# Order of the first transfers, of VectorE's evacuations and of a few steps between experts in a two-layer hybrid trunk

## The reference, cut to what matters

```python
for l in range(DEPTH):                                   # DEPTH = 2
    h = rmsnorm(x, norm_mix[l])
    qa, ka, va, qb, kb, vb, qi, ki, wi, qc, kc, vc, g = split(h @ w_in[l])
    o_a, o_b, o_c = stick_breaking(...), indexed_top_k(...), sliding_window(...)
    gates = sigmoid(g + b_gate[l])
    merged = gates[0] * (o_a @ w_pa[l]) + gates[1] * (o_b @ w_pb[l]) + gates[2] * (o_c @ w_pc[l])
    x = x + merged @ w_out[l]
    x = x + cross_attention(rmsnorm(x, norm_x[l]), rmsnorm(mem, norm_mem[l]), ...)
    hf = rmsnorm(x, norm_ffn[l])
    x = x + (swiglu(hf, w_gu_dense, w_down_dense) if l % 2 == 0 else
             moe_swiglu(hf, w_router, w_gu_moe, w_down_moe))   # sum over 8 experts, top 2 per token
```

## Time and profile before

| | |
|---|---|
| median of 3 runs | 1813.37 us (1812.16 to 1819.61) |
| the profiled execution | 1814.6 us, of which the profile's span is 1813.0 us |
| PE busy | 1717.1 us, 95% of the span, mean granted clock 0.984 |
| DVE busy | 1405.6 us, 78% |
| ACT busy | 1112.3 us, 61% |
| POOL busy | 93.7 us, 5% |
| DMA | 498 MB, 275 GB/s over the span |
| experts (about 800 us to the end) | 56% of the span |

### The profile page before, as it was taken

One profiled execution on the slowest core, in us unless ns is written; L12 is line 12 of the kernel. 1 busy time (PEld: TensorE's weight loads), 2 busy tenths in 40 slices (PEclk: granted clock), 3 DMA queues, 4 the chain that ended last, 5 costly groups with the idle time before them and its releaser, 6 DMA issues.

```text
span 1813.0 us, 22257 instructions
## 1 busy us (share of the span) xinstructions
PE 1717.1 (95%) x7776; PEld 1373.4 (76%) x7776; DVE 1405.6 (78%) x1258; ACT 1112.3 (61%) x1006; POOL 93.7 (5%) x68
## 2 busy tenths in 40 slices
PE   6999887999989998879999989999999999999999
PEld 5877666788768676667888878888788888788776
DVE  5798675554477967748888878888888888888897
ACT  4646354444345453537777777777777777877765
POOL 1200000000003000010000000000000000000440
PEclk9999998999999999979999999999999999999999
DMA  8533592555445325409999989999999999999985
GB/s 288 206 107 135 189 349 93 186 184 185 162 140 204 134 104 186 186 22 397 365 361 380 366 314 387 364 380 368 346 390 362 369 387 366 367 362 366 402 328 203
DMA packets 73791, 498.13 MB, mean 275 GB/s; under 512 B 8192, under 2 KB 8960, under 8 KB 17552
## 3 DMA queue, kind: packets, MB, share of 16 engines
q1 hardware_dynamic: 66000, 466.55, 67.9%
q0 software_dynamic: 7328, 29.87, 4.6%
q10 hardware_dynamic: 416, 1.08, 0.2%
HBM read 481.73 MB, written 15.73 MB: 274 GB/s over the span
## 4 chain that ended last, share of the span: by engine, by line
PE 77%; DVE 11%; ACT 4%; issue 3%; DVEq 3%; DMA 2%; ACTq 0%; SPq 0%; POOLq 0%
PE ps L516 24%; PE ps L520 24%; PE ps L512 24%; DVE w_lo L397 3%; DVE w_lo L901 1%; ACT w_hi L392 1%; PE ps L701 1%; DMA raw<-in_layer_tiles 1%; PE ps L1201 1%; DVE hT_lo L505 1%; DVE st L1447 1%; ACT w_hi L831 1%; DVEq L1450 1%; ACT scratch L1366 0%; DMA z<-rows_of_experts 0%
## 5 line engine op out<-in xcount | busy, mean ns | idle before, releaser
L512 PE MATMUL ps<-w_hi,hT_hi 128*128 128x512 f32 (+1 forms) x1552 | 436.5, 404 | 33.6 <-ACT hT_hi L500 10.6
L901 DVE TENSOR_TENSOR w_lo<-raw,w_hi 128x2048 fp32r<-128x2048 f32 x168 | 391.3, 2331 | 64.2 <-ACT w_hi L831 64.2
L901 DVE TENSOR_TENSOR w_lo<-z,w_hi 128x2048 fp32r<-128x2048 f32 x168 | 386.6, 2305 | 57.1 <-ACT w_hi L831 56.1
L516 PE MATMUL ps<-w_hi,hT_lo 128*128 128x512 f32 (+1 forms) x1552 | 424.3, 396 | 0.8 <-DVE hT_lo L505 0.4
L520 PE MATMUL ps<-w_lo,hT_hi 128*128 128x512 f32 (+1 forms) x1552 | 422.2, 394 | 0.7 <-DVE w_lo L397 0.7
L512 PEld LDWEIGHTS ps<-w_hi,hT_hi 128*128 128x128 f32 x1552 | 278.8, 190 | 96.7 <-ACT hT_hi L500 12.5
L516 PEld LDWEIGHTS ps<-w_hi,hT_lo 128*128 128x128 f32 x1552 | 290.9, 189 | 73.0 <-DVE hT_lo L505 4.1
L831 ACT ACTIVATE w_hi<-z 128x2048 fp32r<-128x2048 f32 x168 | 321.3, 1915 | 39.9 <-PE ps L520 36.2
L520 PEld LDWEIGHTS ps<-w_lo,hT_hi 128*128 128x128 f32 x1552 | 291.0, 189 | 71.2 <-DVE w_lo L397 1.6
L831 ACT ACTIVATE w_hi<-raw 128x2048 fp32r<-128x2048 f32 x168 | 321.1, 1912 | 25.5 <-PE ps L520 25.5
L397 DVE TENSOR_TENSOR w_lo<-raw,w_hi 128x2048 fp32r<-128x2048 f32 (+2 forms) x111 | 243.5, 2203 | 105.0 <-ACT w_hi L392 104.5
(11 more groups left out here) (260 smaller groups left out, 977.5 us busy)
## 6 DMA issues: line engine op xcount, KB each, us to landing
z<-in_moe_tiles SPq DMA_DIRECT2D x168, 1024.0 KB, 6.5
raw<-in_moe_tiles SPq DMA_DIRECT2D x168, 1024.0 KB, 6.5
raw<-in_layer_tiles SPq DMA_DIRECT2D x68, 1024.0 KB, 4.9
raw<-in_dense_tiles SPq DMA_DIRECT2D x33, 1024.0 KB, 4.8
rows_of_experts<-z POOLq DMA_DIRECT2D x1, 8704.0 KB, 37.8
raw<-in_layer_tiles SPq DMA_DIRECT2D x8, 512.0 KB, 3.6
z<-rows_of_experts POOLq DMA_DIRECT2D x8, 512.0 KB, 10.2
rows_of_experts<-z POOLq DMA_DIRECT2D x7, 512.0 KB, 8.1
```

Source lines behind the costliest of these rows:

```text
L512: pe.matmul(acc, hi[:, k, cols], wh, start=start and j == 0, stop=False)
L516: pe.matmul(acc, lo[:, k, cols], wh, start=False, stop=False)
L901: v.tensor_tensor(w_lo[:, ring, :], moe_raw(p), w_hi[:, ring, :].bitcast(F32), ALU.subtract) \
```

## The change

- The identity goes first on SP's queue, then the left half of x's columns, slot 0, the right half, slots 1 and 2, the other five constants, the memory. ACT issues the gains alone. PE waits for the identity, then for each half of x ahead of its transposes, and for the other constants ahead of the fifth slot of `in`.
- In `dve_linear` and `dve_merge` the low halves go up to one slot less before tile 0's evacuation, and the last one stands between the evacuations of tile 0 and of tile 1.
- `dve_merge` signals the left half of the merged rows by its own semaphore; PE turns it without waiting for the right half.
- ACT's Exp of the gates moves into expert 0 (after the first rows' high half); `dve_last` and PE's two transposes move between experts 0 and 1; ACT's copy moves into expert 1, ahead of its store hook.
- POOL issues the last row load ahead of the wait for the last store. What the wait guarded is done by a new transfer of two values into `rows_all`.

```diff
         def sp_program(sp):
-            sp.dma_start(consts[:, :, :], ...).then_inc(sem("const_in"), 16)
+            def load_x(h):
+                cols = slice(h * NB, (h + 1) * NB)
+                sp.dma_start(x_sb[:, :, cols], ...[:, :, cols]).then_inc(sem(f"x{h}_in"), 16)
+            sp.dma_start(ident, t["c_tiles"][0]).then_inc(sem("ident_in"), 16)
+            load_x(0)
             ...
                     load_slot(sp, s)
+                    if s == 0:
+                        load_x(1)
                     if s == RING - 1:
+                        sp.dma_start(consts[:, 1:, :], ...).then_inc(sem("const_in"), 16)
                         load_memory(sp, 0)
@@ pool_moe
             pool.wait_ge(sem("rows_T"), n_it)
+            load_rows(pool, n_it)
             pool.wait_ge(sem("rows_put"), n_it * 16)
-            load_rows(pool, n_it)
+            pool.dma_start(rows_all[0:1, 0:2], expert_rows[bass.ds(n_it * P - P, 1), 0:2]).then_inc(sem("rows_all"), 16)
             (four indirect gathers)
+            pool.wait_ge(sem("rows_all"), 16)
@@ dve_linear
-                ahead(dve_split_to, v, cnt, last, limit)
+                ahead(dve_split_to, v, cnt, last - 1, limit)
                 blk = blk0[name, l] + b
                 v.wait_ge(sem("tile0_done"), blk + 1)
                 take(b, 0).then_inc(sem("evac"), 1)
+                ahead(dve_split_to, v, cnt, last, limit)
                 v.wait_ge(sem("mm_done"), last + 1)
                 take(b, 1).then_inc(sem("evac"), 1)
@@ dve_merge
-                    dve_split_to(v, cnt, min(last + RING, lim))
                     blk = blk0[name, l] + b
                     for i in range(TT):
+                        dve_split_to(v, cnt, min(last + RING - 1 + i, lim))
                         ...
-            ins.then_inc(sem("merged"), 1)
+                    if j == 2:
+                        ins.then_inc(sem(("merged_half", "merged")[b]), 1)
@@ pe_program
-                pe.wait_ge(sem("merged"), l + 1)
-                pe_turn(pe, "mrg", xn)
+                pe_turn(pe, "mrg", xn, halves_in=(("merged_half", l + 1), ("merged", l + 1)))
@@ pe_moe (and alike in dve_moe, with dve_last)
-            for par in range(2):
-                pe_expert(pe, 0, par)
+            pe_expert(pe, 0, 0)
             pe.wait_ge(sem("last_hot"), 1)
             (two transposes)
             ins.then_inc(sem("last_T"), 1)
+            pe_expert(pe, 0, 1)
@@ act_expert, hook
                 if what == "first rows":
                     act_rows_hi(act, 1, 0)
+                    act.wait_ge(sem("top_two"), 1)
+                    act.activation(g2[:, 0:2], g2[:, 0:2], ACT.Exp).then_inc(sem("gate_exp"), 1)
                 elif what == "y":
-                    if not (isinstance(ip, int) and ip == 0):
+                    if isinstance(ip, int):
+                        act.wait_ge(sem("last_T"), 1)
+                        act.activation(last_to_token, ps[:, 7, 0:2 * P], ACT.Copy).then_inc(sem("last_to_token"), 1)
+                    else:
                         act.wait_ge(sem("rows_put"), n * 16)
@@ act_moe
-            (Exp and copy between expert 1 and the loop)
@@ act_program
-            act.dma_start(x_sb[:, :, :], ...).then_inc(sem("x_in"), 16)
             act.dma_start(gains[:, :], t["gain_tiles"]).then_inc(sem("gains"), 16)
```

More of the change, by code:

```diff
@@ L153, in build @@
         n_iter = sb("n_iter", [1, 2], I32)
+        rows_all = sb("rows_all", [1, 2], F32)
         idx8 = sb("idx8", [P, TT, 8], U32)
@@ L249, in sp_program @@
         def sp_program(sp):
-            sp.dma_start(consts[:, :, :], t["c_tiles"].rearrange("i p n -> p i n")).then_inc(sem("const_in"), 16)
+            def load_x(h):
+                cols = slice(h * NB, (h + 1) * NB)
+                sp.dma_start(x_sb[:, :, cols], t["x"][0].rearrange("(t p) d -> p t d", p=P)[:, :, cols]).then_inc(sem(f"x{h}_in"), 16)
+            sp.dma_start(ident, t["c_tiles"][0]).then_inc(sem("ident_in"), 16)
+            load_x(0)
             for l in range(L):
@@ L257, in sp_program @@
                     load_slot(sp, s)
+                    if s == 0:
+                        load_x(1)
                     if s == RING - 1:
+                        sp.dma_start(consts[:, 1:, :], t["c_tiles"][1:].rearrange("i p n -> p i n")).then_inc(sem("const_in"), 16)
                         load_memory(sp, 0)
@@ L466, in wait_evac, with pe_turn @@
                 pe.wait_ge(sem(by), count)
-        def pe_turn(pe, name, src, nchunk=KC, blk=None):
+        def pe_turn(pe, name, src, nchunk=KC, blk=None, halves_in=None):
             for half in range(2):
+                if halves_in is not None:
+                    pe.wait_ge(sem(halves_in[half][0]), halves_in[half][1])
                 if blk is not None:
@@ L881, in act_moe @@
                 act_expert(act, 0, par)
-            act.wait_ge(sem("top_two"), 1)
-            act.activation(g2[:, 0:2], g2[:, 0:2], ACT.Exp).then_inc(sem("gate_exp"), 1)
-            act.wait_ge(sem("last_T"), 1)
-            act.activation(last_to_token, ps[:, 7, 0:2 * P], ACT.Copy).then_inc(sem("last_to_token"), 1)
             act.wait_ge(sem("routed"), 1)
@@ L941, in dve_moe @@
         def dve_moe(v):
-            for par in range(2):
-                dve_expert(v, 0, par)
+            dve_expert(v, 0, 0)
             dve_last(v)
+            dve_expert(v, 0, 1)
             n_pair = v.value_load(n_iter[0:1, 1:2], min_val=N_EXP // 2, max_val=N_EXP)
@@ L1206, in pe_program @@
         def pe_program(pe):
-            pe.wait_ge(sem("const_in"), 16)
+            pe.wait_ge(sem("ident_in"), 16)
             for l in range(L):
@@ L1211, in pe_program @@
                     pe.wait_ge(sem("ffn_added"), l)
-                if l == 0:
-                    pe.wait_ge(sem("x_in"), 16)
-                pe_turn(pe, "mix", x_sb)
+                    pe_turn(pe, "mix", x_sb)
+                else:
+                    pe_turn(pe, "mix", x_sb, halves_in=(("x0_in", 16), ("x1_in", 16)))
                 pe_linear(pe, "in", l, h_ready="mix", part=(0, 4))
@@ L1218, in pe_program @@
                 pe_turn(pe, "mem", mem_n)
+                if l == 0:
+                    pe.wait_ge(sem("const_in"), 16)
                 pe_linear(pe, "in", l, part=(4, 8))
@@ L1375, in act_program @@
             cnt = Count()
-            act.dma_start(x_sb[:, :, :], t["x"][0].rearrange("(t p) d -> p t d", p=P)).then_inc(sem("x_in"), 16)
             act.dma_start(gains[:, :], t["gain_tiles"]).then_inc(sem("gains"), 16)
```

## The result

| | before | after |
|---|---|---|
| median | 1814.01 us (1812.16 to 1819.61, 4 runs) | 1788.72 us (1787.55 to 1790.19, 4 runs) |
| ratio | | 0.9854, 95% interval 0.9837 to 0.9871 |
| profiled execution, its span | 1814.6, 1813.0 us | 1788.05, 1786.5 us |
| PE busy | 1717.1 us, 95% | 1706.8 us, 96% |
| table loads of ACT in the experts | 8 | 1 |

Predicted were 1788.0 us and 25.9 us of gain; the medians differ by 25.3 us, the two profiled spans by 26.5 us. A table load is ACT's instruction ACT_TABLE_LOAD, 1.28 us long; in the experts it stands in front of the Exp and of what follows it, and where the loop returns. To see where the gain lies I took the start of the same PE instruction in both traces at the ends of these stretches and subtracted. Each row gives what was gained since the row above.

What follows compares the result with a forecast made beforehand. PE, busy throughout mid-expert at full clock, bounds the kernel, with waits at six places. Gains summing to 25.9 us took the profiled 1814.6 to 1788.7; with the median 1.2 lower it predicted 1788.0, range 1781 to 1799.

Steps and rivals of the forecast that it cites:

- the six places: PE's waits: start, first `in` block, pa/pb/pc with `out`'s start, middle of `out`, boundary behind expert 1, last row transposes.
- 1, first transfers: At the start, the first low product (L516) comes at 17.9 instead of 19.99 us: gain 2.1, bounds 0.6 and 4.4.
- rival d: At the start, the right half of x lands at the late bound (12.8 us) or after: 1790 to 1791, chance 0.15.
- in proportion that gives 12.8 us: At the start, late bound for x's right half, scaled by bytes to 2.16 MB; 11.3 us was taken.
- The walk from the landing to L516's counterpart: At the start, transposes, a gain multiplication and two low halves after x's right half lands: 6.6 us.
- 2 and 3, low halves and merged half: Gains in layers 0 and 1: first `in` block 1.4 and 1.0 us, pa/pb/pc through `out` 5.3 and 6.3.
- the walk over the six blocks: In pa/pb/pc, by DVE's durations: first wait gone, then waits of 1.7 and 0.9 us, last addition 2.9 us earlier.
- Rivals a and b: a: low halves between evacuations become PE's wait, about 1822, chance 0.02; b: waits only move, 10 us gained, chance 0.10.
- 4, between experts: Boundary behind expert 1 gains 6.3 us, less 0.4 for the loop's count, 0.3 and 0.2: net 5.4 us.
- Table loads out of the loop: In the expert loop, entry with Silu removes both loads and PE's 0.45 us wait in two returns: gain 0.9 us.
- Rival c: In the expert loop, the table loads stay in each round: 1.4 us less gained, 1789.4 us, chance 0.15.
- 5, last rows: Last expert's row transposes: the load goes some 120 us earlier, gain 3.5 us, bounds 1.9 and 3.6.

Runs made afterwards that it cites:

- s_x_act: The changed kernel with both halves of x on ACT's queue ahead of the gains, identity and slots on SP's; one execution, 1790.66 us.
- s_quiet_xf: The changed kernel with both halves of x ahead of slot 0 and POOL's five small first transfers about 30 us later; one execution, 1782.62 us.
- p_experts: The kernel before with only the last expert's one-hot and its Exp moved into the first two experts; 1804.44 us, ratio 0.9937.
- p_rows: The kernel before with only the last expert's row load ahead of POOL's wait for the stored rows; 1812.55 us, ratio 0.9983.
- exp_again: The changed kernel with an extra, unread Exp of 128x2 values on ACT between expert 1 and the loop; one execution, 1788.48 us.
- rows_off: The changed kernel with the last rows loaded behind the wait for the stored rows again; 1788.61 us, ratio to before 0.9847.
- p_lows: The kernel before with only the low halves between the evacuations, merged rows still turned after both halves; 1800.43 us, ratio 0.9924.
- s_undo: The changed kernel with the first transfers as they were before; 1785.58 us, ratio to before 0.9847.

## Why the prediction was right, and where it wasn't

**Bounds of the kernel.** Right. All that was gained was gained at the six places, in the loop's first chunk and returns, and in the two cross-attentions. But the prediction counted only idle time. Behind long waits the profile of before also has products at the half clock (1.7 us behind expert 1 and 1.6 in the last row chunk). The prediction has them in its distances from transpose to transpose, without a name.

**1, first transfers (+2.1, measured -0.6 here, 0 over eight executions).** The term was mis-sized, by more than its bounds (0.6 to 4.4), and rival d had its place: the right half landed at the late bound or after (12.98 to 13.95). The step that failed is "in proportion that gives 12.8 us": it takes bytes for the measure of time at the start. It left POOL's broadcasts in the place they had, with "nearer to the late end" as the allowance. They cost 1.8 to 2.7 us (right half at 12.98 to 13.95 with them, 11.22 without). The walk from the landing to L516's counterpart was right to 0.1 us (its four terms add up to 6.5, measured 6.62).

The page "DMA: Bandwidth & Descriptors" of the Trainium skill (Specifications) wants at least 512 bytes for a transfer at the full rate and says that below it the engines read, modify and write. The head gains' broadcasts are of 256 bytes a row (32 KB over 128 rows), and the trace agrees as far as it goes: 188 GB/s with them, 417 without; no run changes the size of the pieces alone. The same page (Queues, rings and completion order, Arbitration) says that each DMA engine goes round the queues that have work, a packet at a time; by that rule small pieces get as many turns as large ones, and x on ACT's queue gets no precedence. `s_x_act` agrees (16.19). The fixed cost of about 2 us for each transfer, which the prediction set against cutting x in two, is not seen as a loss: in `s_quiet_xf` the halves land at 7.07 and 8.40, and PE turns both without a break.

**2 and 3, low halves and merged half (14.0, measured 13.8 in this pair of profiles).** The mechanism is right, and so was the walk over the six blocks: a wait of 1.7 for bank 7 (1.65) and one of 0.9 (0.47). In layer 1 two errors meet: the `in` part gave 1.5 instead of 1.0, the middle 5.6 instead of 6.3. The 6.3 isn't the sum of what the text gives for it (4.1, about 1.9, less 0.2: 5.8, near the 5.6). And the size is that of one execution of before; against `p_experts` and `p_rows` the middles gain up to 9.0 us each, since their clock falls behind the same waits. Rivals a and b fell: no block pays its low half to PE as a new loss, and what was gained in front of `xq` is still there at the experts.

**4, between experts (5.4, measured 6.1).** "I charge PE 0.4 for the loop's count" was too much: 0. Of the 0.3 and 0.2 that it charges between experts 0 and 1, 0.2 in all is seen. **Table loads out of the loop (0.9, measured 1.9):** each return costs 0.7, not the 0.45 of its one visible wait: from start to start the wait costs 0.61, since the groups of products otherwise overlap by 0.16, and the group behind it takes 0.10 longer; and the first entry costs another 0.5, which the prediction didn't count. Rival c fell: the trace shows one load in the experts, at the first Silu. The page "ScalarE activation tables: per-element evaluation and per-set limits" (Table sets in the compiler and the runtime) has them placed per block; the trace agrees only in part: no inner loop has one here, and `exp_again` shows that the body gets its two only if it is entered with another table than it ends with.

**5, last rows (3.5, measured 3.7 in this pair of profiles).** Right by the two traces, but not a fixed gain, and none seen on top of the other parts (`rows_off`). The prediction took one execution's wait for a property of the kernel, and its step "the load is issued some 120 us earlier" is wrong: POOL issues in order, the store of the expert before stands in front, so the load goes out 0.77 us behind that store, some 8 us earlier than before. That is enough. The claim "POOL's adding: 0, within 1 us" held (-0.5).

**Not foreseen:** +1.3 and +0.8 in the cross-attentions. The runs don't show them as an effect of the change: the last section has them for the same code.

So 1788.0 came out because errors cancelled, which is luck: the start was 2.7 too high, POOL's adding 0.5 and parts 2 and 3 0.2; the experts with the last rows were 1.9 and the cross-attentions 2.1 too low. A small slip belongs to it: 1788.7 less 1.2 is 1787.5, not 1788.0. And 13.8 and 3.7 of the gain are differences to one profile of before, which other profiles of the same code move by 1.6 to 6.3 and by 3.7 us.

## What to carry to other kernels

Count a start by its pieces, not by its bytes: put off small broadcasts until the urgent transfers have landed, and don't count on a second queue for precedence. Between two evacuations there is room for one long step of an engine, if you count what PE still has to do in the other bank; but ask also who waits behind that step on the third engine. A wait of TensorE can cost more than its idle time: look at the granted clock behind it. A wait that stands in one profile once is a property of that execution until a second profile shows it.

## What the runs showed of the hardware

**The same code takes 3 us more or less by TensorE's clock.** From the scores to the first product of `xo` in layer 0 the order of work is the same in all fourteen kernels. It took 22.9 us before, 21.6 after, and between 19.8 (`p_lows`) and 22.8 in the others, without relation to the edit: 20.1 in `exp_again`, 22.8 in `rows_off`, whose code up to there is the same. Timeline and stretch of the kernel before:

```profile
271.13 5.36 PE L1186 MATMUL ps<-headsT 128*128 128x256 f32 x16 [1.11 <-ACT headsT L1360]
```

```profile
270.00:275.00 5.00, 3.89 (x11) 3.19 (x11) 4.36 (x8) 4.01 (x5) 0.00 (x0) 0.66 0.11 46
```

and of the changed kernel:

```profile
264.95 3.72 PE L1200 MATMUL ps<-headsT 128*128 128x256 f32 x16 [1.11 <-ACT headsT L1375]
```

```profile
264.00:269.00 5.00, 3.72 (x16) 2.96 (x16) 4.28 (x9) 3.88 (x5) 0.00 (x0) 1.00 0.47 173
```

In the one the granted clock is at 0.66 in this stretch, a mean of full speed (2.4 GHz) and its half (1.2 GHz), and the 16 score products take 5.4 us; in the other it is at full speed and they take 3.7. Ahead of them PE had waited 1.6 and 1.1 us in both. In both kernels it is down a little later as well. When the fall comes differs from execution to execution, and that decides which products lie in it. It is also most of why `s_undo` could be 2.2 us faster outside the start: behind a wait of 1.86 us in layer 1's mixers (1.85 in `s_undo`) the clock is at 0.72 from 626 to 632 us in the changed kernel and at 1.00 in `s_undo`, which makes 1.3 us. In layer 0, 0.65 us more is PE's wait for `out`'s last evacuation, whose slot came late.

**One product's start doesn't measure a start.** Of the three executions with the changed start the low product is latest in the changed kernel (20.57, against 19.60 in `rows_off` and 19.88 in `exp_again`), yet pa starts first there (193.01, 193.52, 193.71). The two groups of four products behind it took 1.54 and 1.10 us in the changed kernel, and 1.91 each, which is the half clock, in the other two. `s_quiet_xf` is 3.3 to 4.2 us ahead of the three at the low product and 3.4 to 4.1 at the first product of `out`.

**POOL's adding costs PE 3.1 to 5.8 us, and the clock makes most of the difference.** The chunks beside it, summed over 8.61 each, gave 4.2 before, 4.7 after, 3.1 in `p_rows`, 3.2 in `exp_again`, 5.8 in `p_lows`, with the same instructions. The clock stays at 1.00 beside it in before, `p_rows` and `exp_again`. In the changed kernel it is at 0.50 from 1704 to 1706 us, behind a wait of 2.27; in `p_lows` at 0.57 from 1712 to 1720. DVE's low halves then take up to 4.5 instead of 2.3 us.
